# Hybrid encoder trunk: in attention the weighted sum over values issued after the transposes of a step instead of before them

## The reference

```python
s = einsum('bqhd,bkhd->bhqk', qn, k_nope) + einsum('bqhr,bkr->bhqk', qr, k_rope)
p = softmax(s * MLA_SCALE, axis=-1)
o = einsum('bhqk,bkhd->bqhd', p, v)
```

## Time and profile before

| | us |
|---|---|
| median of the runs (lowest, highest of 3) | 852.72 (852.43, 853.53) |
| the profiled execution | 853.92 |
| its span, first to last instruction | 852.1 |
| PE busy, of the span | 767.0 (90%) |
| DVE busy | 417.1 (49%) |
| ACT busy | 333.3 (39%) |
| POOL busy | 195.8 (23%) |

### The profile page before, as it was taken

The page is one execution under the profiler, slowest core; times in us unless marked ns, Lnnn a source line. Parts: engine busy times, 40 slices in busy tenths (PEclk is TensorE's granted clock), DMA queues, the critical chain, the costliest instruction groups (busy, mean ns, idle before and its releaser), DMA issues. The chain is left out here.

```text
span 852.1 us, 14303 instructions
## 1 busy us (share of the span) xinstructions
PE 767.0 (90%) x5936; PEld 637.4 (75%) x5936; DVE 417.1 (49%) x699; ACT 333.3 (39%) x570; POOL 195.8 (23%) x223
## 2 busy tenths in 40 slices
PE   3899999999999999998845899999999947999996
PEld 2786778788888878887744688888888845788885
DVE  5734766475565310000771566666667746433332
ACT  6441545334545323111530544444444553233321
POOL 2312125464454212110340000000000026233320
PEclk9999999999999999999676999999999987999999
DMA  7402021011111111400533000000033020444431
GB/s 274 126 12 63 26 95 41 27 40 64 64 50 40 54 65 60 148 23 22 167 100 88 12 13 14 13 20 18 13 106 131 1 98 27 147 149 148 148 123 49
DMA packets 32443, 61.37 MB, mean 72 GB/s; under 512 B 3296, under 2 KB 16000, under 8 KB 32384
## 3 DMA queue, kind: packets, MB, share of 16 engines
q1 hardware_dynamic: 26384, 46.36, 16.9%
q10 hardware_dynamic: 6000, 14.16, 4.3%
HBM read 42.42 MB, written 17.69 MB: 71 GB/s over the span
## 5 line engine op out<-in xcount | busy, mean ns | idle before, releaser
L77 PE MATMUL psum<-h_hi,z_w_hi 128*128 128x512 f32 x432 | 174.4, 404 | 3.8 <-DVE h_lo L697 3.8
L79 PE MATMUL psum<-h_hi,z_w_lo 128*128 128x512 f32 x432 | 169.0, 391 | 0.0
L78 PE MATMUL psum<-h_lo,z_w_hi 128*128 128x512 f32 x432 | 168.8, 391 | 0.0
L77 PEld LDWEIGHTS psum<-h_hi,z_w_hi 128*128 128x128 f32 x432 | 81.5, 189 | 24.3 <-DVE h_lo L697 4.6
L79 PEld LDWEIGHTS psum<-h_hi,z_w_lo 128*128 128x128 f32 x432 | 81.4, 189 | 17.6
L78 PEld LDWEIGHTS psum<-h_lo,z_w_hi 128*128 128x128 f32 x432 | 81.6, 189 | 16.4 <-issue 0.7
L1544 ACT ACTIVATE a_weights<-psum,a_bias,mla_q_scale 128x1024 f32<-128x1024 f32 (+1 forms) x48 | 51.1, 1064 | 103.8 <-DVE a_bias L1583 103.8
L77 PE MATMUL psum<-o_w_hi,o_m_hi 128*128 128x512 f32 x192 | 76.7, 400 | 15.4 <-DVE o_w_lo L1871 14.4
L78 PE MATMUL psum<-o_w_lo,o_m_hi 128*128 128x512 f32 x192 | 75.8, 395 | 0.0
L79 PE MATMUL psum<-o_w_hi,o_m_lo 128*128 128x512 f32 x192 | 75.7, 394 | 0.0
L1607 DVE TENSOR_TENSOR a_turned_lo<-psum,a_turned_hi 128x512 fp32r<-128x512 f32 x80 | 52.3, 687 | 41.7 <-ACT a_turned_hi L1561 41.7
(11 more groups left out here) (212 smaller groups left out, 1493.2 us busy)
## 6 DMA issues: line engine op xcount, KB each, us to landing
z_w_raw<-in_w_z_dram SPq DMA_DIRECT2D x17, 512.0 KB, 3.4
n_x_in<-in_x_dram SPq DMA_DIRECT2D x12, 512.0 KB, 4.1
gates_scratch<-z_gate ACTq DMA_DIRECT2D x24, 256.0 KB, 2.0
o_x_in<-in_x_dram SPq DMA_DIRECT2D x12, 512.0 KB, 3.5
out_dram<-o_y ACTq DMA_DIRECT2D x12, 512.0 KB, 2.6
o_w_raw<-in_w_out_dram SPq DMA_DIRECT2D x8, 512.0 KB, 9.6
a_q_rope<-rope_scratch SPq DMA_DIRECT2D x12, 256.0 KB, 2.6
o_gate_first<-gates_scratch SPq DMA_DIRECT2D x6, 512.0 KB, 5.3
```

Of the source, the lines that this page charges most:

```text
L77: nc.tensor.matmul(out, a_hi, b_hi, start=first, stop=False)
L78: nc.tensor.matmul(out, a_hi, b_lo, start=False, stop=False)
L79: return nc.tensor.matmul(out, a_lo, b_hi, start=False, stop=last)
```

## The change

In each of the three streams the piece for the values is moved behind the piece for the turn, within the same step. PE issues scores, project, turn, values, output. ACT does the turned copies ahead of the latent copy, DVE the reciprocal and the turned low parts ahead of the latent low part. The steps (lags) are as before, no instruction is added or taken away, and the numbering of items is the same, since values are not items.

```diff
@@ -1547,10 +1547,6 @@
                       .then_inc(exp_done, 1)
                 for h, b in projected_at(m):
                     project(h, b)
-                for p in pair_at(m, VALUES_LAG):
-                    act.wait_ge(values_done, p + 1)
-                    nc.scalar.activation(latent_hi[:, p % 2, :], psum[:, 6 + p % 2, :PAIR], ACT.Copy)\
-                      .then_inc(latent_hi_ready, 1)
                 if 0 <= m - TURN_LAG < STEPS:
                     tile = m - TURN_LAG
                     p = tile // 2
@@ -1561,6 +1557,10 @@
                         nc.scalar.activation(turned_hi[:, p % 2, 4 * n:4 * n + 4, (tile % 2) * P:(tile % 2 + 1) * P],
                                              psum[:, 4 + item % 2, :].rearrange("p (k q) -> p k q", k=4),
                                              ACT.Copy).then_inc(turned_hi_ready, 1)
+                for p in pair_at(m, VALUES_LAG):
+                    act.wait_ge(values_done, p + 1)
+                    nc.scalar.activation(latent_hi[:, p % 2, :], psum[:, 6 + p % 2, :PAIR], ACT.Copy)\
+                      .then_inc(latent_hi_ready, 1)
 
         @block.vector
         def _(dve):
@@ -1591,11 +1591,6 @@
                                             share_row[:, p % 2, :], ALU.mult).then_inc(gathered, 1)
                 for h, b in projected_at(m):
                     project(h, b)
-                for p in pair_at(m, VALUES_LAG):
-                    dve.wait_ge(latent_hi_ready, p + 1)
-                    nc.vector.tensor_tensor(latent_lo[:, p % 2, :], psum[:, 6 + p % 2, :PAIR],
-                                            latent_hi[:, p % 2, :].bitcast(F32), ALU.subtract)\
-                      .then_inc(latent_lo_ready, 1)
                 if 0 <= m - TURN_LAG < STEPS:
                     tile = m - TURN_LAG
                     dve.wait_ge(exp_done, tile + 1)
@@ -1606,6 +1601,11 @@
                               slice((tile % 2) * P, (tile % 2 + 1) * P))
                         nc.vector.tensor_tensor(turned_lo[at], psum[:, 4 + item % 2, :].rearrange("p (k q) -> p k q", k=4),
                                                 turned_hi[at].bitcast(F32), ALU.subtract).then_inc(turned_lo_ready, 1)
+                for p in pair_at(m, VALUES_LAG):
+                    dve.wait_ge(latent_hi_ready, p + 1)
+                    nc.vector.tensor_tensor(latent_lo[:, p % 2, :], psum[:, 6 + p % 2, :PAIR],
+                                            latent_hi[:, p % 2, :].bitcast(F32), ALU.subtract)\
+                      .then_inc(latent_lo_ready, 1)
 
         @block.tensor
         def _(pe):
@@ -1674,10 +1674,10 @@
                     scores(m)
                 for h, b in projected_at(m):
                     project(h, b)
+                if 0 <= m - TURN_LAG < STEPS:
+                    turn(m - TURN_LAG)
                 for p in pair_at(m, VALUES_LAG):
                     values(p)
-                if 0 <= m - TURN_LAG < STEPS:
-                    turn(m - TURN_LAG)
                 for p in pair_at(m, OUTPUT_LAG):
                     output(p)
```

## The result

| | before | after |
|---|---|---|
| median (lowest, highest), us | 853.12 (852.43, 853.59), 4 runs | 882.52 (881.23, 884.29), 4 runs |
| ratio, 95% interval | | 1.035 (1.0336 to 1.0364) |
| profiled execution, us | 853.92 | 881.23 |
| its span | 852.1 | 879.4 |
| first scores to last output's start in the attention stage | 464.31 to 693.61 = 229.3 | 463.49 to 722.90 = 259.4 |

The profiled execution after is the shortest of its four, and the one before is 0.8 longer than its median, so the traces differ by 27.3 us where the medians differ by 29.4. In the traces the stage is 30.1 longer; its start is 0.8 earlier, and what follows it is 2.0 shorter (158.5 to 156.5).

A forecast was written before the change was run, and what follows sets the result against it. PE was taken to bound the attention stage, waiting for DVE's low parts. Waits of 24.05 us plus 4.8 for clock falls make 28.9; added to the median 852.72 this gives 881.6 us, range 874 to 890.

The forecast's parts named there:

- Part 1: Project steps: the turn's second bank waits for a_q_lo, 2.67 us long, 1.71 short, 7.05 per head with projections.
- P: Start of the projection on PE in a project step; a_q_lo was forecast 3.78 us after it, 2.82 in short steps.
- Part 2: Odd steps without a project: the turn waits 0.60 us or more for turned low parts; head 3 in all +2.15.
- step 4's wait: PE's wait of 0.66 us in a head's step 4, forecast to go because the values now stand between.
- Part 3: Attention stage, long project steps: PE's clock falls behind the waits, three falls of 1.6 us, 4.8 in all.
- the fall after 418.39: Clock at 1.2 GHz in 422 to 423, after one-column matmuls and transposes; cited as agreeing that transposes do not hold it.
- the rule taken strictly: Transposes do not count as busy for the clock: all six long project steps fall, sum 33.6 in place of 28.9.
- The rival with none or one fall: Attention stage: waits as forecast, clock never or once down, 876.8 to 878.4 us; chance 0.28.
- the one with six or more falls: Attention stage: waits as forecast and six or more clock falls, 886.4 to 891.2 us; chance 0.15.
- a hidden wait: Project steps: the wait for a_q_lo is mostly hidden, DVE or ACT reaching the projection sooner, 855 to 863 us; chance 0.05.
- no change: Attention stage: ring-bound steps dominate and PE's waits only change place, 852.7 us; chance 0.03.
- a gain: Attention stage: the earlier turn removes PE's waits for low parts, 10.3 us, giving 842.4; chance 0.04.

The follow-up runs named there:

- e2: New order in the nine project steps only, all other steps in the order of before: 880.49 us, 1.0327 of the kernel before.
- e1: The nine project steps keep the order of before, every other step has the new order: 854.37 us, 1.0026 of the kernel before.
- e10: Changed kernel with extra transposes on PE between the two banks of a turn in project steps: 873.90 us, 1.0247 of the kernel before.
- e7: Kernel before, with turned copies (steps without values) and a_q_hi ahead of ACT's exponential, a_q_lo ahead of DVE's gather: 838.25 us, ratio 0.9825.
- e4: New order on PE alone, ACT and DVE keep the order of before: 885.35 us, 1.0375 of the kernel before.
- e6: Changed kernel with a_q_hi ahead of ACT's exponential and a_q_lo ahead of DVE's gather: 863.55 us, 1.0131 of the kernel before.

## Why the prediction was right, point by point

- **Part 1, the project steps.** Predicted: second bank at P+4.61 and P+3.65, 21.2 us for the nine. Measured: `a_q_lo` at P+3.77, second bank at P+4.51; in a short step P+3.55 (514.44 to 517.99). The tenth of difference is the handover, which I had taken from a turn behind a turned low part (0.83), while here it is 0.74. e2's stage is 27.9 longer than before (463.64 to 720.80, less 229.3) and has five falls; less five times 1.5 that is some 20.
- **Part 2, the other odd steps.** Predicted 2.9, of which head 3 was 2.15. e1's stage is 231.85 (463.85 to 695.70), +2.55; head 3 in the changed kernel, from its first scores (661.24) to the last output, is 61.66 against 59.65, +2.0. As forecast, step 4's wait is gone and step 3's has come for it (0.8 in place of 1.0). In head 3 the turns of steps 5 and 7 come 0.86 and 0.59 late (the view prints 0.69 and 0.42), at the lower end of the forecast 0.6 to 1.1.
- **Together.** Predicted 24.05 for the waits; the traces give 30.1 - 7.7 = 22.4.
- **Part 3, the clock.** That the clock would fall behind the long waits was right, the size was too small and one of the reasons wrong. I chose three falls of 1.6 (4.8), by halving six and from nothing measured; the profiled execution had five of 1.5 (7.7). I had named 3.55 us with transposes and no other matmul as the cause, and the fall after 418.39 as a witness. e10 says that transposes hold the clock as matmuls do, so what lies behind a fall is the wait. And the witness was misread: what L1361 issues there are ordinary matmuls against an identity (`nc.tensor.matmul`), not `nc.tensor.transpose`, and the clock fell within 1 us of their start at 420.99, right behind 2.6 us of one-column matmuls (granted clock 1.00 in 420 to 421, 0.81 in 421 to 422, 0.50 in 422 to 423). Whether the one-column matmuls did it no experiment here tried. The rule of the Trainium skill, "TensorE: Matmul & The Clock Gate", Part 4, that transposes do not count as busy for the clock, differs from e10, where float32 transposes of 128 columns held it at full rate; the measurement decides. The fall after 418.39 neither agrees with that rule, as the prediction had it, nor speaks against it. (The view prints these as MATMUL; that they are transposes is taken from the kernel's `nc.tensor.transpose`.) By the rule taken strictly the sum would have been 33.6 in place of 28.9; the medians differ by 29.4.
- **The rest of the kernel.** I took 0; the traces have -2.8. 1.5 to 2 of it is again the clock: the earlier trace rows have a fall at 715 in the output stage, at the same place of which (about 745) the trace after has none. Ahead of the stage the trace before has a fall at 432 to 435 that the trace after lacks, too. No run shows that the change had a part in that.
- **The sum.** 852.72 + 28.9 = 881.6 against 882.52: two terms, the waits 1.6 too long and the clock 2.9 too short, offset each other in part. That leaves 1.3 missing in the stage (30.1 in the traces); 0.7 of it is gone again in the rest (29.4), and the runs before beside the changed kernel were 0.4 above the 852.72 that I started from. A miss of 0.9 us is partly luck; the two terms are off by 1.6 and 2.9. The rival with none or one fall is refuted by the trace; the one with six or more falls is one fall away from it. The rivals of a hidden wait, of no change and of a gain fell with the second bank at P+4.51.
- **What I had missed.** I treated the exponential's place ahead of the copies as given. Its place cost time in both orders: with the turned copies ahead of it, e7 takes 14 us from the kernel before.

Open: how many falls an execution has. The four times of the changed kernel lie between 881.23 and 884.29, two falls apart, and only one of them has a trace. That the number varies within one kernel is likely from e4: its quickest run (881.12 us) had a mean granted clock of 0.966, the traced one (884.93, three falls in the stage) 0.961.

## What to carry to other kernels

When a piece of work is moved, look for who shares a buffer with its new neighbour: the turn did not need the projection's data, only its bank, and the values between the two were the time in which the bank came free. Before moving work on the bound engine to cover a round trip, see what stands ahead of the round trip's copies in the other engines' queues; here a 1.2 us exponential that PE hardly waited for (0.6 us, once) stood ahead of 0.6 us copies that PE waited for again and again. A wait of 2.4 us on PE can cost 1.5 more behind it through the clock, so a cover that is lost is to be priced with that.

## What the runs showed of the hardware

- Waits of 2.4 us between two short groups of transposes dropped PE's clock from 2.4 to 1.2 GHz in five of six cases, for 3.4 us each, at 1.5 us of time; waits of 1.4 us did not in three of three, nor did those of up to 1.0 in e6. Whether a given long wait did so was not the same in each kernel: e2 had five, e4 three.
- Work without use inside the wait held the clock at full rate, with matmuls of 256 columns or with transposes: 9 us less for the kernel.
- The waits that the view prints for PE are shorter than the delay they stand for, by some 0.16 each: 0.37 in the first row, where scores and wait took 2.86 (540.08 to 542.94) against 2.33 in e7 (531.65 to 533.98); 1.00 against 1.17 in the earlier trace rows.
